# Attention periods of a hybrid encoder step: kept whole between dense steps, one turning each, and raw keys loaded earlier

## What is computed

```python
def sb_block(q, q_pos, k, v):
    z = jnp.einsum('bqhd,bkhd->bhqk', q, k).astype(jnp.float32) * (SB_DH ** -0.5)
    mask = k_pos[None, :] < q_pos[:, None]
    lk = jnp.where(mask, jax.nn.log_sigmoid(-z), 0.0)
    ...                     # after: for each key, the sum of lk over the keys later than it
    A = jnp.exp(jnp.where(mask, jax.nn.log_sigmoid(z) + after, -jnp.inf))
    return jnp.einsum('bhqk,bkhd->bqhd', A.astype(v.dtype), v)

# per layer
out = jnp.concatenate([go, so, co], axis=-1) @ w_out          # so: the attention's rows
x = layer_norm(DEEPNORM_ALPHA * x + mix, ln1_g[l], ln1_b[l])
ff = jnp.square(jax.nn.relu(x @ w_up[l])) @ w_down[l]
x = layer_norm(DEEPNORM_ALPHA * x + ff, ln2_g[l], ln2_b[l])
```

## Time and profile before

| | |
|---|---|
| median of three runs | 3315.71 us |
| the profiled execution | 3317.47 us, span 3315.6 us |
| TensorE (PE) busy | 2802.1 us, 85% |
| VectorE (DVE) busy | 1734.9 us, 52% |
| ScalarE (ACT) busy | 1074.0 us, 32% |
| GpSimd (POOL) busy | 330.7 us, 10% |
| mean granted TensorE clock | 0.915 |

### The profile page before, as it was taken

The page is one execution under the profiler, slowest core; times in us unless marked ns, Lnnn a source line. Parts: engine busy times, 40 slices in busy tenths (PEclk is TensorE's granted clock), DMA queues, the critical chain, the costliest instruction groups (busy, mean ns, idle before and its releaser), DMA issues. The chain is left out here.

```text
span 3315.6 us, 37193 instructions
## 1 busy us (share of the span) xinstructions
PE 2802.1 (85%) x13838; PEld 2308.9 (70%) x13838; DVE 1734.9 (52%) x2463; ACT 1074.0 (32%) x1783; POOL 330.7 (10%) x283
## 2 busy tenths in 40 slices
PE   5999999756643768989887989988899998899997
PEld 4778789645532656767776777767677776789895
DVE  5333431189844555545567555556755543754445
ACT  3333332234433333333323333332343332222231
POOL 1100100176000000000001000001100000100000
PEclk9999999857875879989998999989899998999998
DMA  5444543313246423333333333332334332232221
GB/s 187 154 160 159 174 153 119 103 62 106 72 123 207 146 64 100 107 104 96 122 99 115 110 124 104 104 117 91 112 119 133 95 94 96 83 108 78 77 87 57
DMA packets 320626, 374.99 MB, mean 113 GB/s; under 512 B 24225, under 2 KB 203601, under 8 KB 320449
## 3 DMA queue, kind: packets, MB, share of 16 engines
q1 hardware_dynamic: 296224, 329.21, 31.9%
q10 hardware_dynamic: 18832, 26.10, 2.1%
q0 software_dynamic: 5392, 17.31, 1.5%
HBM read 309.49 MB, written 63.05 MB: 112 GB/s over the span
## 5 line engine op out<-in xcount | busy, mean ns | idle before, releaser
L111 PE MATMUL p_ps_u<-p_xh,p_wh 128*128 128x512 f32 (+1 forms) x1280 | 470.5, 368 | 5.3 <-DVE p_xl L1589 5.3
L111 PE MATMUL p_ps_d<-p_wh,p_hh 128*128 128x512 f32 (+1 forms) x1088 | 445.5, 409 | 21.6 <-DVE p_res L1540 19.4
L112 PE MATMUL p_ps_u<-p_xh,p_wl 128*128 128x512 f32 (+1 forms) x1280 | 462.7, 361 | 0.0
L113 PE MATMUL p_ps_u<-p_xl,p_wh 128*128 128x512 f32 (+1 forms) x1280 | 461.6, 361 | 0.0
L1540 DVE SCALAR_TENSOR_TENSOR p_res<-p_res,p_ps_d 128x512 f32<-128x512 f32 (+1 forms) x340 | 231.9, 684 | 413.3 <-PE p_ps_d L113 391.4
L112 PE MATMUL p_ps_d<-p_wh,p_hl 128*128 128x512 f32 (+1 forms) x1088 | 434.6, 399 | 0.0
L113 PE MATMUL p_ps_d<-p_wl,p_hh 128*128 128x512 f32 (+1 forms) x1088 | 433.7, 399 | 0.0
L1449 ACT ACTIVATE p_wh<-p_wst 128x1024 fp32r<-128x1024 f32 x288 | 294.1, 1049 | 221.7 <-PE p_ps_d L113 157.6
L1596 DVE TENSOR_TENSOR p_r<-p_r 128x512 f32<-128x512 f32 (+1 forms) x160 | 97.2, 607 | 490.5 <-ACT p_hh L1479 490.4
L1565 DVE TENSOR_TENSOR p_wl<-p_wst,p_wh 128x1024 fp32r<-128x1024 f32 x288 | 345.3, 1222 | 10.9 <-ACT p_wh L1449 10.6
L1472 ACT ACTIVATE p_r<-p_ps_u 128x512 f32<-128x512 f32 (+1 forms) x160 | 83.7, 523 | 636.1 <-PE p_ps_u L113 632.0
(11 more groups left out here) (155 smaller groups left out, 4476.1 us busy)
## 6 DMA issues: line engine op xcount, KB each, us to landing
p_wst<-in_w_up SPq DMA_DIRECT2D x128, 512.0 KB, 4.3
p_wst<-in_w_down SPq DMA_DIRECT2D x128, 512.0 KB, 3.7
p_wst<-in_w_in SPq DMA_DIRECT2D x128, 256.0 KB, 3.6
p_kk<-ks_scratch SPq DMA_DIRECT2D x84, 256.0 KB, 5.0
p_vv<-vs_scratch SPq DMA_DIRECT2D x84, 256.0 KB, 4.6
p_wst<-in_w_out SPq DMA_DIRECT2D x32, 512.0 KB, 3.9
zt_scratch<-p_outb ACTq DMA_DIRECT2D x48, 256.0 KB, 2.0
p_wst<-in_w_in SPq DMA_DIRECT2D x32, 264.0 KB, 3.3
```

Of the source, the lines that this page charges most:

```text
L111: pe.matmul(out, lhs_hi, rhs_hi, start=first, stop=False, skip_group_check=skip)
L112: pe.matmul(out, lhs_lo, rhs_hi, start=False, stop=False, skip_group_check=skip)
L113: return pe.matmul(out, lhs_hi, rhs_lo, start=False, stop=last, skip_group_check=skip)
```

## The change

Four edits of the planner; no engine's instructions change. An item of 128-row tiles is due a whole period after the one before it (the sample's 64-row items keep the half). `periods` now holds the borders of the periods, `add_attention` counts in periods instead of list entries, and so lays out whole periods everywhere. Where two weighings stand in one period and the first ends a head, that head's `o_out` stands right behind it. `p_load` of a block comes one block earlier: block 2 behind the first `p_store`, and block c + 2 behind `p_store` of c.

```diff
@@ -1090,11 +1090,10 @@
         for u, _, _ in items:
-            at = max(units[u]["slot1"] + 1, at + 0.5)
+            at = max(units[u]["slot1"] + 1, at + (1.0 if units[u]["tiles"][0][1] == P else 0.5))
             due.append(int(at))
-        attention, head_end, periods = [], {}, []
+        attention, head_end, periods = [], {}, [0]
         for n in range(due[-1] + 2):
-            periods.append(len(attention))
...
-            attention += [("turn", k) for k in turns[:1]] + [("weigh", k) for k in weighs]
+            attention += [("turn", k) for k in turns[:1]]
+            for k in weighs:
+                j = units[items[k][0]]["head"]
+                attention.append(("weigh", k))
+                if k + 1 == heads[j]["item1"] and k != weighs[-1]:
+                    attention.append(("o_out", j))
+                    head_end[j] = n + 1
...
-            for k in weighs:
+            for k in weighs[-1:]:
                 j = units[items[k][0]]["head"]
                 if k + 1 == heads[j]["item1"]:
                     attention.append(("o_out", j))
-                    head_end[j] = len(attention)
+                    head_end[j] = n + 1
...
+            periods.append(len(attention))
...
         def add_attention(upto):
             nonlocal put
-            order.extend(attention[put:upto])
-            put = max(put, upto)
+            if upto > put:
+                order.extend(attention[periods[put]:periods[upto]])
+                put = upto
...
-        order += [("p_load", 0), ("q_load", 0), ("p_load", 1), ("pk", 0, 0), ("pk", 0, 1), ("pv", 0), ("p_store", 0), ("q_prep", 0), ("k_load", 0)]
+        order += [("p_load", 0), ("q_load", 0), ("p_load", 1), ("pk", 0, 0), ("pk", 0, 1), ("pv", 0), ("p_store", 0), ("p_load", 2), ("q_prep", 0), ("k_load", 0)]
         steps = []
         for c in range(1, 6):
-            steps += [[("pk", c, 0)], [("pk", c, 1)], [("pv", c)], [("p_store", c)] + ([("p_load", c + 1)] if c < 5 else [])]
+            steps += [[("pk", c, 0)], [("pk", c, 1)], [("pv", c)], [("p_store", c)] + ([("p_load", c + 2)] if c < 4 else [])]
         for n, x in enumerate(steps):
-            add_attention(max(i for i in periods if i <= group_end[0] * (n + 1) // (len(steps) + 1)))
+            add_attention(group_end[0] * (n + 1) // (len(steps) + 1))
             order += x
...
             if i < mixed[-1]:
-                add_attention(begun + int((len(attention) - begun) * spent / sum(price)))
-        assert put == len(attention) and next_w == len(wunits)
+                add_attention(begun + int((len(periods) - 1 - begun) * spent / sum(price)))
+        assert put == len(periods) - 1 and next_w == len(wunits)
```

## The result

The changed kernel takes 3134.47 us (median of four runs, 3130.47 to 3136.55) against 3315.99 us of the kernel before beside it: ratio 0.945, 95% interval 0.9433 to 0.9466. The profiled execution has a span of 3134.2 us, 181.4 less than before, and a mean granted clock of 0.935 instead of 0.915.

A forecast was written before the change was run, and what follows sets the result against it. The planner's order, not an engine's total, was taken as the bound. Idle 103 + clock 50 + lead-in 5 = 158 us off 3317.5 gave 3159, or 3157 as a median; range 3095 to 3245.

The forecast's parts named there:

- ln2 stretches: Mixed part, four layer norms within four ups after a group's turn: of 25 us of waits 18 kept, 7 gained.
- Idle time: TensorE's idle time saved in the mixed part: 113 + 7 − 7 − 10 = 103 us.
- steady waits: Mixed part: TensorE's waits before turnings, weighings and z that whole, single-turning periods remove, 113 us.
- small new waits: Mixed part: 10 us left for places with two weight splits and for the query split late in a period.
- The sample's end: Last five periods, 64-row heads: two turnings each without a dense step between, 17 us of waits, 7 lost.
- The pause: Before the first group's transposes: 15.4 us wait before a turning stays, effect 0, between −6 and +6.
- Clock: Mixed part: time regained from half clock as waits go, about half their length, 50 us, ends 0 and 116.
- Lead-in: 955 to 1109.2 us: earlier raw loads, an extra period and second turnings, net 5 us saved, between −6 and +15.
- Head of queue: Rival, chance 0.04: each scan holds VectorE's queue until its sigmoid and additions pile up; slower, 3386 us.
- Half comes back: Rival, chance 0.18: VectorE late in most up stretches, 1 us waits return 75 us; about 3235 us.
- Not what it says: Rival, chance 0.04: uneven spacing lets two periods meet without a dense step; no change, about 3310 us.
- More goes: Rival, chance 0.16: VectorE keeps up in ln2 and at the sample's end, no small waits; about 3100 us.

The follow-up runs named there:

- the kernels of the table: The kernel before, the changed kernel and the follow-up kernels, each with mixed-part idle and clock loss listed; medians from 3093.5 to 3456.8 us.
- due times alone: The kernel before with only the changed due times and the `o_out` placement they need, list still cut anywhere, loads as before: 3274.12 us, ratio 0.9865.
- whole periods alone: The changed kernel with the old due times and old loads, periods still laid out whole: 3456.8 us, ratio 1.0421.
- in pairs: The changed kernel with its whole periods laid two by two, no dense step between the two of a pair: 3422.61 us, ratio 1.0312.

## Why the prediction was right, point by point

The time (3134.5 against 3157) lies in the forecast case, 3120 to 3200, and every sign held: the turnings' waits are below 50 us and 21.4 of the 22.9 stand in the ln2 stretches and the sample's heads, the clock is 0.97, and the end kept its length to 2.1 us. The sum was 158 us and the difference is 181.4; 15.4 us more idle time and 10.7 us that were not foreseen make up the lack.

- *Idle time, forecast 103, measured 118.4.* The 113 us of steady waits went whole. Two terms for what stays were sized too high. The small new waits, put at 10, are 3.4 (1.5 before a turning, 1.9 before z): the margins of 1.5 and 0.3 us held nearly everywhere. The ln2 stretches, of which 18 us were kept, hold 4.3 and 5.8. The sample's end agrees partly by luck: 17 forecast and 17.3 there, but the five second turnings wait only 13.1 of it, and 4.2 are a weighing that waits for `ob`, which the prediction did not name. The pause kept its 14.1 (15.4), the out starts their 14.0 (14.6). With the two corrections the sum is 103 + 6.6 + 7.9 = 117.5.
- *Clock, forecast 50, measured 49.6.* The number agrees because two errors cancel: the idle time was forecast too low and the rate a little too high, 50 / 103 against 0.42 us per us of idle time that went. The upper end, 116, could not be reached: it took the clock's lack over the idle time too, and all that was lost before is 78.8. Over the kernels of the table the lost time is 0.29 to 0.47 of the idle time.
- *Lead-in, forecast 5, measured 4.5.* The wait for raw keys turned into one for the stores, as forecast. The extra period and the second turnings together come to nothing: 144.4 us with and without them; what each does is not shown.
- *Not foreseen: 10.7 us* of the mixed part that are neither idle nor at half clock. TensorE has the same matmuls there less five (one period moved to the lead-in, some 1.5 us). The rest is not settled; the same figure is 1376.1 with due times alone, 1373.9 with whole periods alone and 1367.5 with both.
- *The account of the cause.* The prediction named three things: both turnings in one period, one bank, and a list cut between turning and `lo`. Its first edit, though, was credited with taking the second turning's wait away ("now waits for a `lo` issued a period before"). Due times alone show that this is not enough: there the `lo` of a period before is still late, since a dense step stands ahead of it and none behind. It takes both edits.
- *The rivals.* "Head of queue": the scans wait 12.7 us in 94, about 0.14 us each, where 1.05 us of TensorE time per period would have decided, and TensorE's waits for VectorE's additions are 14.0 us in the mixed part, nearly all around ln1. "Half comes back": 3.4 us of small waits, not 75. "Not what it says": 8 of 143 turnings have no dense step since the last `lo`, five with the sample and three in the pause, and one border has a single down, 2.7 us, where the prediction had never less than 5.4. Were it so in general, it would not be "no change", as that rival had it, but a slower kernel, as with whole periods alone or in pairs. "More goes" came true in part, by the ln2 stretches and the small waits.

## What to carry to other kernels

In a list that all engines walk in order, a long step pays as cover only if it stands between the release of a resource (here `lo`, which frees the bank) and the next claim on it, not between claim and release: keep claim and release on one side of it. Such an edit has parts that alone are worth little or do harm, so price the order that results, not each edit. When one wait goes, look in the queue of the DMA issuer for the next one: here the sample's keys were late as soon as the turnings' waits were gone.

## What the runs showed of the hardware

The query split on VectorE (128x256, both inputs in SBUF) takes more than twice as long in the changed kernel. By form in the mixed part, before and after:

```profile
L1619 DVE TENSOR_TENSOR p_ql<-p_qraw,p_qh 128x256 fp32r<-128x256 f32 x23 | 11.9, 515 | 0.0
```

```profile
L1626 DVE TENSOR_TENSOR p_ql<-p_qraw,p_qh 128x256 fp32r<-128x256 f32 x22 | 24.0, 1089 | 0.0
```

One of them in the timeline of the changed kernel, beside POOL:

```profile
1285.03 1.09 POOL L1685 TENSOR_TENSOR p_aw<-p_sg,p_keep 128x512 f32<-128x512 f32 x1 [17.06 <-DVE p_keep L1641]
...
1285.45 0.95 DVE L1626 TENSOR_TENSOR p_ql<-p_qraw,p_qh 128x256 fp32r<-128x256 f32 x1
```

With whole periods it always runs beside POOL's `mul`. It overlaps it from 1285.45 to 1286.12, 0.67 us, and 0.28 are left after that. All 22 are so: duration less overlap is 0.28 us, whatever the overlap (0.67 to 1.01 us). Before, 6 of 23 met POOL for 0.25 us or more and kept the same 0.28; 16 did not meet it and took 0.42, and one met it for its first 0.08 us and took 0.41. So, but for a first 0.14 us (0.42 less 0.28), it seems to stand still while POOL runs. (The 128x64 splits of the sample fit less well: two that start within 0.1 us of a `mul` take 0.21, as they do alone.) The Trainium skill (SBUF — State Buffer, "Terms") says that VectorE and GpSimd share a port pair by an exclusive lock and that the loser blocks fully; the 128x256 splits agree, but for the first 0.14 us. It cost 12 us of VectorE time that the prediction did not count; TensorE's waits for `ql` in the mixed part did not grow by it (5.3 us against 5.2). `lo`, which reads one input from PSUM, keeps its 0.67 us.
